# Running the delta rule's chunk scan between the levels of the block inverses, one chunk per level

## Chip, cores and metric

The kernel runs on one core of one Trainium2 chip, as one launch. The time is device microseconds (us) of the whole program, the median over several executions.

## What is computed

The program is one inference step of a hybrid encoder trunk with two layers, for 512 prompt frames and 64 sample frames at once (576 columns). Layer 0 is: SwiGLU feed-forward, then a mixer of 4 gated-delta heads and 4 latent-attention heads, then a second feed-forward. Layer 1 has a state-space mixer in place of the first. The change lies in the gated-delta part of the mixer. It works in chunks of 64 frames: 8 of the prompt, whose state starts at zero, and one of the sample, whose state is an input. The reference for one chunk, for all heads:

```python
def gdn_chunk_step(s0, inp):
    q, k, v, beta, g = inp
    ...
    sol = lax.linalg.triangular_solve(lower + jnp.eye(C, dtype=lower.dtype), rhs,
                                      left_side=True, lower=True, unit_diagonal=True)
    dv = v.shape[-1]
    u = sol[..., :dv] - jnp.einsum('bhtk,bhkv->bhtv', sol[..., dv:], s0)
    o = (gam[..., None] * jnp.einsum('bhtk,bhkv->bhtv', q, s0)
         + jnp.einsum('bhts,bhsv->bhtv', jnp.einsum('bhtd,bhsd->bhts', q, k) * decay, u))
    g_end = G[..., -1:]
    s_new = (jnp.exp(g_end)[..., None] * s0
             + jnp.einsum('bhsk,bhsv->bhkv', jnp.exp(g_end - G)[..., None] * k, u))
    return s_new, o
```

The triangular solve needs no state and can be done for all chunks alike. `u`, `o` and `s_new` need the state that the chunk before left.

## The kernel before

Every engine has one instruction stream, written out by hand, and waits on semaphores; each engine runs its stream strictly in the order written. Around the change TensorE (PE) runs `gdn_tensor`, then `scan_tensor`, then `onorm_tensor`; VectorE (DVE) and ScalarE (ACT) run the functions of the same stages.

**The block inverses** (`gdn_tensor`, `gdn_scalar`, `gdn_vector`). The 576 frames are five blocks: four of 128 frames (two chunks each) and block 4 of 64 frames (the sample). `PAIRS_OF_BLOCKS` takes them as pair one (blocks 0 and 1), pair two (blocks 2 and 3) and block 4 alone. For each block `gram` builds products and transposes, and the inverse of the block's triangular matrix is built in `LEVELS = 6` levels. In a level from 1 to 5, for each block of the pair, `first_product` (L1045) multiplies on PE, ACT copies the result to SBUF (`ys`, L1110), `updates` (L1054, L1058) multiplies again, and DVE subtracts from two running matrices and makes the mask product of the next level (`xi`, `zi`, `cm`: L1182, L1183, L1159). PE issues the first products of both blocks, then the updates of both. The last level leaves L1058 out. Then `solution` (L1073, L1075) makes what the scan needs, into PSUM banks 3 and 4, and ACT copies it out as `uv` and `wt` (L1115, L1116). The levels use banks 5 to 7 for one block of the pair and 0 to 2 for the other; `gram` uses banks 0 to 4.

**The scan** (`scan_tensor`, `scan_vector`, `scan_scalar`) starts when all blocks are done (`all_blocks_done`). For each of nine chunks, with four heads in each group of matmuls: L1214 multiplies `wt` with the state `st`; DVE makes `uu` from it (L1242); L1222 starts the chunk's output from the state; L1225 multiplies `kd` with `uu`; DVE makes the next state (L1247, four instructions); L1229 adds the rest of the output; ACT copies the output to `og` (L1265). Two sets of banks alternate from chunk to chunk (0 and 1, 2 and 3, 4 and 5). The trace counts each float32 matmul twice, so four heads stand as x8.

```python
            pe.wait_ge(s_st, c + 1)
...
            for h in range(HEADS):
                m = pe.matmul(ps[r0:r0 + CH, c % 2, h * P:h * P + P], wt[:, 4 * b + h, r0:r0 + CH], st[:, s, h, :],
                              start=True, stop=True)
```

`st` and `uu` lie over arrays of the first block set, which is why the scan waits for all blocks, and GpSimd (POOL) loads the sample's state into `st` after the blocks too (L827). After the scan, `onorm_*` normalises `og`, and latent attention, the output projection and the rest of the trunk follow.

Of the kernel before, what the change touches and what calls it, by code (L numbers as in the profile page):

```python
# [17 lines left out]
F32 = mybir.dt.float32  # L18
# [5 lines left out]
P = 128  # L24
# [15 lines left out]
NS = 3  # L40
# [70 lines left out]
def trunk(nc, i, o):  # L111
# [640 lines left out]
    assert RM0 + 2 * BYTES <= W0 and 2 * BYTES <= 2 * PADW * 4 and BYTES <= TOKENS * 4  # L752
    st = nc.alloc_sbuf_tensor_at("st", [P, 2, HEADS, P], F32, offset=KP0)
    uu = nc.alloc_sbuf_tensor_at("uu", [P, 2, HEADS, P], F32, offset=KP0 + 4096)
    rn = nc.alloc_sbuf_tensor_at("rn", [P, TOKENS], F32, offset=KP0 + 4096)
# [63 lines left out]
    def mix_gpsimd(pool):  # L819
        wait_u(pool, 1)  # L820
        pool.dma_start(xp[:, :, SEQ + 3:SEQ + 6], i["conv_state"]).then_inc(s_mc, 16)
        pool.dma_start(ckv[:, TOKENS:KEYS], i["cache_latent"]).then_inc(s_mk, 16)
        pool.wait_ge(s_evac, g_in + 6)
        pool.dma_start(o["conv_p"], xp[:, :, SEQ:SEQ + 3]).then_inc(s_out, 16)
        pool.dma_start(o["conv_s"], xp[:, :, PADW - 3:PADW]).then_inc(s_out, 16)
        all_blocks_done(pool)
        pool.dma_start(st[:, 1, :, :], i["gdn_state"]).then_inc(s_s0, 16)  # L827
        pool.wait_ge(s_st, 10)
        pool.dma_start(o["gdn_p"], st[:, 0, :, :]).then_inc(s_out, 16)
        pool.dma_start(o["gdn_s"], st[:, 1, :, :]).then_inc(s_out, 16)  # L830
        mla_gpsimd(pool)
# [175 lines left out]

    def all_blocks_done(eng):
        eng.wait_ge(s_bd[0], 3)
        eng.wait_ge(s_bd[1], 2)  # L1010

    def gdn_tensor(pe):
# [105 lines left out]
    def gdn_vector(dve):  # L1118
# [67 lines left out]

        for blocks in PAIRS_OF_BLOCKS:
# [12 lines left out]
    def chunk(c):  # L1200
        b = c // 2
        r0 = (c % 2) * CH
        return b, r0, 1 if c == 8 else 0

    def scan_tensor(pe):
        all_blocks_done(pe)
        for c in range(9):
            b, r0, s = chunk(c)
            tok = slice(c * CH, c * CH + CH)
            pe.wait_ge(s_st, c + 1)  # L1210
            if c == 8:
                pe.wait_ge(s_s0, 16)
            for h in range(HEADS):
                m = pe.matmul(ps[r0:r0 + CH, c % 2, h * P:h * P + P], wt[:, 4 * b + h, r0:r0 + CH], st[:, s, h, :],  # L1214
                              start=True, stop=True)
            m.then_inc(s_sw, 1)
            if c >= 2:
                pe.wait_ge(s_oc, c - 1)
            out = lambda h: ps[:, 2 + c % 2, h * CH:h * CH + CH]

            for h in range(HEADS):
                pe.matmul(out(h), st_old(c)[:, h, :], qg[:, h, tok], start=h == 0, stop=False)  # L1222
            pe.wait_ge(s_su, c + 1)
            for h in range(HEADS):
                m = pe.matmul(bank(4 + c % 2)[:, h, :], kd[r0:r0 + CH, 4 * b + h, :], uu[r0:r0 + CH, c % 2, h, :],  # L1225
                              start=True, stop=True)
            m.then_inc(s_ku, 1)
            for h in range(HEADS):
                m = pe.matmul(out(h), uu[r0:r0 + CH, c % 2, h, :], pt[r0:r0 + CH, 4 * b + h, r0:r0 + CH],  # L1229
                              start=False, stop=h == HEADS - 1)  # L1230
            m.then_inc(s_so, 1)

    def scan_vector(dve):
        all_blocks_done(dve)
        dve.memset(st[:, 0, :, :], 0.0).then_inc(s_st, 1)
        for c in range(9):
            b, r0, s = chunk(c)
            dve.wait_ge(s_sw, c + 1)
            if c >= 2:
                dve.wait_ge(s_so, c - 1)  # L1240
            rows_ = slice(r0, r0 + CH)
            dve.tensor_tensor(uu[rows_, c % 2, :, :], uv[rows_, 4 * b:4 * b + 4, :],  # L1242
                              ps[rows_, c % 2, :].rearrange("p (h c) -> p h c", h=HEADS),
                              ALU.subtract).then_inc(s_su, 1)
            dve.wait_ge(s_ku, c + 1)
            for h in range(HEADS):
                ins = dve.scalar_tensor_tensor(out=st[:, s, h, :], in0=st[:, s, h, :], scalar=ge[:, h, c:c + 1],  # L1247
                                               in1=bank(4 + c % 2)[:, h, :], op0=ALU.mult, op1=ALU.add)
            ins.then_inc(s_st, 1)
            if c == 7:  # L1250
                dve.wait_ge(s_s0, 16)
            if c < 8:
                dve.wait_ge(s_st, c + 2)
        dve.wait_ge(s_st, 10)
# [4 lines left out]
    def scan_scalar(act):  # L1259
        act.activation(zg[:, :, :], zg[:, :, :], ACT.Silu).then_inc(s_zs, 1)  # L1260
        for c in range(9):
            act.wait_ge(s_so, c + 1)
            if c == 0:
                all_blocks_done(act)
            act.activation(og[:, :, c * CH:c * CH + CH],  # L1265
                           ps[:, 2 + c % 2, 0:HEADS * CH].rearrange("p (h t) -> p h t", h=HEADS),
                           ACT.Copy).then_inc(s_oc, 1)

# [1100 lines left out]
```

## Time and profile before

| what | value |
|---|---|
| median of 3 runs | 2725.94 us (2725.25 to 2735.22) |
| the profiled execution's own time | 2718.02 us |
| its span, first to last instruction | 2716.4 us |
| PE busy | 2520.6 us, 93% of the span |
| DVE, ACT, POOL busy | 1467.3, 705.3, 134.0 us |
| mean granted clock of PE | 0.937 of full speed |
| block inverses, pair one / pair two / block 4 | about 688 to 748, 748 to 817, 817 to 855 us |
| chunk scan | 855 to 923 us |

The profile gives for each engine the time in which it ran instructions. In the page, a line of 40 digits cuts the span into 40 slices of 68 us; PEclk is the share of full clock that PE was granted in each. "PE 128*128 128x128" is a matmul whose weights are 128 rows by 128 columns and whose moving operand is 128 rows by 128 columns; PEld is the weight load that goes with it and overlaps it. A bracket such as [0.76 <-DVE cm L1159] says how long the engine had been idle before that row and which instruction released it.

### The profile page before, as it was taken

Reading aid. Unit: us, or ns where it says so; the run is one execution under the profiler, and the core shown is the slowest. Engines: PE = TensorE matmul, PEld = TensorE weight load, DVE = VectorE, ACT = ScalarE, POOL = GpSimd, SP = SyncE. Lnnn points to the kernel's source line nnn. Section 1 sums busy time; section 2 is a strip of 40 time slices with the busy share of each in tenths; the row PEclk is TensorE's granted clock in tenths of the full one; section 3 lists DMA queues with packets and bytes.
Section 4 is the critical chain, followed back from the end, with each engine's and each line's share of the span. In section 5 each row is a group of like instructions: output and inputs, shape, how many; then the busy total and the mean of one; then the engine's idle time right before and its main releaser. Section 6 shows DMA issues by size and latency. Waiting matters only on the chain.

```text
span 2716.4 us, 40923 instructions
## 1 busy us (share of the span) xinstructions
PE 2520.6 (93%) x18002; PEld 2407.2 (89%) x18002; DVE 1467.3 (54%) x2370; ACT 705.3 (26%) x940; POOL 134.0 (5%) x199
## 2 busy tenths in 40 slices
PE   6999999997777889999999999999977999999997
PEld 6999999995666656899999999999966889999996
DVE  4677664752552333586367487677765436333333
ACT  3121211533111132421121241222243315111112
POOL 2000000200000000100000020000000002000001
PEclk9999999997785568999999999999988999999998
DMA  6445442220000001244334234333324212222211
GB/s 266 167 152 194 176 154 74 80 75 16 1 1 4 23 18 62 70 172 168 111 140 153 91 131 177 107 139 137 126 76 124 65 63 78 93 70 86 93 59 55
DMA packets 55871, 275.07 MB, mean 101 GB/s; under 512 B 7216, under 2 KB 17008, under 8 KB 33040
## 3 DMA queue, kind: packets, MB, share of 16 engines
q1 hardware_dynamic: 40608, 186.35, 19.6%
q0 software_dynamic: 13648, 82.82, 8.6%
q8 instruction: 141, 2.31, 0.3%
q10 hardware_dynamic: 1440, 3.32, 0.3%
q14 instruction: 34, 0.28, 0.0%
HBM read 259.13 MB, written 13.32 MB: 100 GB/s over the span
## 4 chain that ended last, share of the span: by engine, by line
PE 60%; DVE 4%; ACT 1%; issue 1%; DMA 1%; SPq 1%; POOL 0%; ACTq 0%; DVEq 0%
PE ps L271 47%; PE ps L278 3%; PE ps L489 2%; PE ps L472 1%; DVE x L589 1%; PE ps L1395 1%; PE ps L1225 1%; PE ps L1214 1%; PE ps L1222 1%; PE ps L1394 1%; SPq L1687 1%; PE ps L1229 1%; DMA wm<-output_matrices 1%; DVE ln_rstd_tail L585 1%; PE ps L1416 0%
## 5 line engine op out<-in xcount | busy, mean ns | idle before, releaser
L271 PE MATMUL ps<-u_hi,w_hi 128*128 128x288 f32 x3040 | 648.5, 295 | 2.4 <-DVE w_lo L263 1.4
L271 PE MATMUL ps<-u_hi,w_lo 128*128 128x288 f32 x3040 | 647.2, 294 | 0.0
L271 PE MATMUL ps<-u_lo,w_hi 128*128 128x288 f32 x3040 | 647.0, 294 | 0.0
L263 DVE TENSOR_TENSOR w_lo<-w_raw,w_hi 128x2048 fp32r<-128x2048 f32 (+3 forms) x184 | 360.6, 1960 | 389.1 <-ACT w_hi L255 385.0
L255 ACT ACTIVATE w_hi<-w_raw 128x2048 fp32r<-128x2048 f32 (+3 forms) x184 | 303.4, 1649 | 897.2 <-DMA w_raw<-in_w_in 421.0
L271 PEld LDWEIGHTS ps<-u_hi,w_hi 128*128 128x128 f32 x3040 | 488.3, 188 | 3.2 <-DVE w_lo L263 1.6
L271 PEld LDWEIGHTS ps<-u_lo,w_hi 128*128 128x128 f32 x3040 | 488.0, 188 | 0.0
L271 PEld LDWEIGHTS ps<-u_hi,w_lo 128*128 128x128 f32 x3040 | 487.9, 188 | 0.0
L611 DVE SCALAR_TENSOR_TENSOR ada_out<-ada_w,c_act 128x1024 f32<-128x1024 f32 x272 | 317.0, 1221 | 28.9 <-DMA ada_w<-in_w_ada 26.9
L271 PE MATMUL ps<-h_lo,w_hi 128*128 128x288 f32 x1392 | 293.5, 295 | 0.0
L271 PE MATMUL ps<-h_hi,w_hi 128*128 128x288 f32 x1296 | 281.2, 298 | 4.8 <-DVE h_lo L1886 4.8
L271 PE MATMUL ps<-h_hi,w_lo 128*128 128x288 f32 x1296 | 276.7, 295 | 0.0
L415 DVE TENSOR_TENSOR hf<-ps,sg 128x576 f32<-128x576 f32 x88 | 66.6, 757 | 298.3 <-ACT sg L398 298.3
L271 PEld LDWEIGHTS ps<-h_lo,w_hi 128*128 128x128 f32 x1392 | 222.7, 189 | 0.0
L271 PEld LDWEIGHTS ps<-h_hi,w_hi 128*128 128x128 f32 x1296 | 210.0, 189 | 7.1 <-DVE h_lo L1886 5.0
L271 PEld LDWEIGHTS ps<-h_hi,w_lo 128*128 128x128 f32 x1296 | 208.6, 189 | 0.0
L398 ACT ACTIVATE sg<-ps 128x576 f32<-128x576 f32 x88 | 57.2, 650 | 488.1 <-PE ps L271 479.2
L441 DVE SCALAR_TENSOR_TENSOR x<-ps,res_gate,x 128x224 f32<-128x224 f32 (+2 forms) x240 | 85.9, 412 | 118.5 <-PE ps L271 95.2
L278 PE MATMUL ps<-u_hi,w_hi 128*128 128x288 f32 x352 | 109.4, 311 | 8.2 <-POOL u_lo L553 8.2
L278 PE MATMUL ps<-u_lo,w_hi 128*128 128x288 f32 x352 | 104.7, 297 | 0.0
L278 PE MATMUL ps<-u_hi,w_lo 128*128 128x288 f32 x352 | 104.7, 297 | 0.0
L553 POOL TENSOR_TENSOR u_lo<-u_f,u_hi 128x288 fp32r<-128x288 f32 x80 | 70.8, 899 | 440.5 <-ACT u_hi L532 438.7
(376 smaller groups left out, 2707.4 us busy)
## 6 DMA issues: line engine op xcount, KB each, us to landing
w_raw<-in_w_in SPq DMA_DIRECT2D x88, 1024.0 KB, 4.8
ada_w<-in_w_ada POOLq DMA_DIRECT2D x64, 1024.0 KB, 4.9
w_raw<-in_w_out SPq DMA_DIRECT2D x32, 768.0 KB, 4.3
w_raw<-in_w_out SPq DMA_DIRECT2D x32, 640.0 KB, 3.8
w_raw<-in_w_mix_in SPq DMA_DIRECT2D x10, 1024.0 KB, 4.8
ada_w<-in_w_ada SPq DMA_DIRECT2D x8, 1024.0 KB, 26.2
output_matrices<-wm_new POOLq DMA_DIRECT2D x8, 576.0 KB, 3.2
wm<-output_matrices SPq DMA_DIRECT2D x8, 576.0 KB, 5.0
```

The costliest lines, as they stand in the source:

```text
L255: act.activation(w_hi[:, g % NS, 0:WIDTH[g]], w_raw[:, g % NS, 0:WIDTH[g]], ACT.Copy).then_inc(s_whi, 1)
L263: dve.tensor_tensor(w_lo[:, g % NS, 0:WIDTH[g]], w_raw[:, g % NS, 0:WIDTH[g]], w_hi[:, g % NS, 0:WIDTH[g]].bitcast(F32), ALU.subtract).the ...
L271: m = pe.matmul(out[:, a, :], w, mv[:, a, :], start=start and n_ == 0, stop=stop and n_ == 2)
L278: m = pe.matmul(out, w, mv, start=start and n_ == 0, stop=stop and n_ == 2)
L398: act.activation(halves(sg[:, b % 2, :]), pair(2 * (b % 2)), ACT.Silu).then_inc(s_sg, 1)
L415: dve.tensor_tensor(halves(hf[:, b % 2, :]), pair(2 * (b % 2) + 1), halves(sg[:, b % 2, :]), ALU.mult).then_inc(s_evac, 1)
L441: return dve.scalar_tensor_tensor(out=x[:, b, lo:hi], in0=pair(2 * (b % 2))[:, a, lo - a * HALF:hi - a * HALF], scalar=res_gate[:, site, b ...
L472: return pe.matmul(pair(1)[:, a, :], mean_w[:, :], half(x, k, a), start=k == 0, stop=k == KD - 1)
L489: pe.matmul(pair(3)[:, a, :], mean_w[:, :], sq[:, k % SQ, :], start=k == 0, stop=k == KD - 1).then_inc(s_var, 1)
L553: pool.tensor_tensor(half(u_lo, k, a), half(u_f32, k, a), half(u_hi, k, a).bitcast(F32), ALU.subtract).then_inc(s_up, 1)
L585: chains["dve"].step(dve.reciprocal(ln_rstd[:, a, :], ln_std[:, a, :]))
L611: return dve.scalar_tensor_tensor(out=ada_out[:, n % 2, :], in0=w, scalar=1.0, in1=c_act[:, st, :], op0=ALU.mult, op1=ALU.mult, accum_out= ...
```

## The change

The scan is cut into `chunk_state` (L1214 and L1222 of before), `chunk_update`, `chunk_output` (L1225 and L1229 of before), `chunk_next_state` and `chunk_copy`. Chunks 0 to 3 run in levels 1 to 4 of pair two, chunks 4 to 7 in levels 1 to 4 of block 4: on PE the chunk's first half stands between the first products and the updates, its second half after the updates. On DVE `uu` stands before the level's subtractions and the new state after them; on ACT the copy stands after the level's copies. Chunk 8 (the sample) stays behind the last solution. All chunks use bank 3 (state product, then outer product) and bank 4 (output), which the levels leave alone; `solution` waits for the chunks before it writes there. `st` and `uu` move to the upper halves of a weight slot that holds a narrow block at that time, so the state is cleared and the sample's state loaded before the blocks instead of after them.

```diff
-    st = nc.alloc_sbuf_tensor_at("st", [P, 2, HEADS, P], F32, offset=KP0)
-    uu = nc.alloc_sbuf_tensor_at("uu", [P, 2, HEADS, P], F32, offset=KP0 + 4096)
+    M_SLOT = (first["mla"] + 1) % NS
...
+    st = nc.alloc_sbuf_tensor_at("st", [P, 2, HEADS, P], F32, offset=W0 + (M_SLOT + 1) * BLOCK * 4 - 2 * BYTES)
+    uu = nc.alloc_sbuf_tensor_at("uu", [P, 2, HEADS, P], F32, offset=W0 + (NS + M_SLOT + 1) * BLOCK * 4 - 2 * BYTES)
...
-        all_blocks_done(pool)
+        pool.wait_ge(s_blk, g_mla)
         pool.dma_start(st[:, 1, :, :], i["gdn_state"]).then_inc(s_s0, 16)
...
+    def scan_beside(j, lv):
+
+        return 4 * (j - 1) + lv - 1 if j and lv <= 4 else None
+
+    def block_of_chunk_done(eng, c):
+        b = c // 2
+        eng.wait_ge(s_bd[b % 2], b // 2 + 1)
...
         def solution(b, n_, paired):
...
+            if j:
+                pe.wait_ge(s_st, 4 * j + 1)
+                pe.wait_ge(s_oc, 4 * j)
...
             for lv in range(1, LEVELS):
+                c = scan_beside(j, lv)
                 for b, t0, n_ in blocks:
                     first_product(b, n_, lv)
+                if c is not None:
+                    if lv == 1:
+                        pe.wait_ge(s_kv[blocks[-1][0] % 2], j + 1)
+                    chunk_state(pe, c)
                 for b, t0, n_ in blocks:
                     updates(b, n_, lv)
+                if c is not None:
+                    chunk_output(pe, c)
...
+                if scan_beside(j_, lv) is not None:
+                    chunk_copy(act, scan_beside(j_, lv))
...
+        dve.wait_ge(s_blk, g_mla)
+        dve.memset(st[:, 0, :, :], 0.0).then_inc(s_st, 1)
...
             for lv in range(1, LEVELS):
+                c = scan_beside(j, lv)
+                if c is not None:
+                    chunk_update(dve, c)
                 for b, t0, n_ in blocks:
                     update(b, n_, lv)
                     if lv + 1 < LEVELS:
                         part(b, n_, lv + 1)
+                if c is not None:
+                    chunk_next_state(dve, c)
...
+    def chunk_state(pe, c):
+        b, r0, s = chunk(c)
+        tok = slice(c * CH, c * CH + CH)
+        block_of_chunk_done(pe, c)
+        pe.wait_ge(s_st, c + 1)
+        if c == 8:
+            pe.wait_ge(s_s0, 16)
+        for h in range(HEADS):
+            m = pe.matmul(ps[r0:r0 + CH, 3, h * P:h * P + P], wt[:, 4 * b + h, r0:r0 + CH], st[:, s, h, :],
+                          start=True, stop=True)
+        m.then_inc(s_sw, 1)
+        if c >= 1:
+            pe.wait_ge(s_oc, c)
+        for h in range(HEADS):
+            pe.matmul(chunk_out(h), st_old(c)[:, h, :], qg[:, h, tok], start=h == 0, stop=False)
...
     def scan_tensor(pe):
-        all_blocks_done(pe)
-        for c in range(9):
...
+        chunk_state(pe, 8)
+        chunk_output(pe, 8)
```

What this does to the order, at three places. In the rows, names with a number such as `zi_120` belong to the second block of the pair.

PE, one level of pair two, before (first products, updates):

```order
L1045 MATMUL ps<-zi,cm 128x128 x4
L1045 MATMUL ps<-zi_120,cm_122 128x128 x4
L1054 MATMUL ps<-ys,xi 128x128 x4
L1058 MATMUL ps<-xi,ys 128x128 x4
L1054 MATMUL ps<-ys_121,xi_119 128x128 x4
L1058 MATMUL ps<-xi_119,ys_121 128x128 x4
```

and now, with the line numbers of the changed kernel:

```order
L1052 MATMUL ps<-zi,cm 128x128 x4
L1052 MATMUL ps<-zi_120,cm_122 128x128 x4
L1239 MATMUL ps<-st,wt 64x128 x4
L1245 MATMUL ps<-qg,st 128x64 x4
L1061 MATMUL ps<-ys,xi 128x128 x4
L1065 MATMUL ps<-xi,ys 128x128 x4
L1061 MATMUL ps<-ys_121,xi_119 128x128 x4
L1065 MATMUL ps<-xi_119,ys_121 128x128 x4
L1254 MATMUL ps<-uu,kd 128x128 x4
L1258 MATMUL ps<-pt,uu 128x64 x4
```

Sixteen matmuls of a chunk stand inside the level, eight ahead of the updates and eight behind them.

DVE, the same level of pair two, now:

```order
L1269 TENSOR_TENSOR uu<-uv,ps 64x512
L1201 TENSOR_TENSOR xi<-xi,ps 128x512
L1202 TENSOR_TENSOR zi<-zi,ps 128x512
L1178 TENSOR_TENSOR cm<-dl,masks 128x512
L1201 TENSOR_TENSOR xi_119<-xi_119,ps 128x512
L1202 TENSOR_TENSOR zi_120<-zi_120,ps 128x512
L1178 TENSOR_TENSOR cm_122<-dl_118,masks 128x512
L1278 SCALAR_TENSOR_TENSOR st<-st,ge,ps 128x128 x4
```

The six rows in the middle are the level as it was; the first row and the last (four instructions) are the chunk's.

PE, one level of block 4, the last solution and the end of the scan, now:

```order
L1052 MATMUL ps<-zi,cm 64x64 x4
L1239 MATMUL ps<-st,wt 64x128 x4
L1245 MATMUL ps<-qg,st 128x64 x4
L1061 MATMUL ps<-ys,xi 64x64 x4
L1065 MATMUL ps<-xi,ys 64x64 x4
L1254 MATMUL ps<-uu,kd 128x128 x4
L1258 MATMUL ps<-pt,uu 128x64 x4
...
L1083 MATMUL ps<-vp,zi 64x128 x4
L1085 MATMUL ps<-zi,kp 128x64 x4
L1239 MATMUL ps<-st,wt 64x128 x4
L1245 MATMUL ps<-qg,st 128x64 x4
L1254 MATMUL ps<-uu,kd 128x128 x4
L1258 MATMUL ps<-pt,uu 128x64 x4
```

Before, a level of block 4 had its three groups alone, and nine chunks followed the last solution instead of one.

## Rows read from the trace of the kernel before

**Rows 1.** The page: granted clock by slice, and the chain that ended last.

```profile
PEclk9999999997785568999999999999988999999998
...
PE ps L271 47%; PE ps L278 3%; PE ps L489 2%; PE ps L472 1%; DVE x L589 1%; PE ps L1395 1%; PE ps L1225 1%; PE ps L1214 1%; PE ps L1222 1%; PE ps L1394 1%; SPq L1687 1%; PE ps L1229 1%; DMA wm<-output_matrices 1%; DVE ln_rstd_tail L585 1%; PE ps L1416 0%
```

**Rows 2.** Busy time by stretch: us, PE, PEld, DVE, ACT, POOL, PEclk, DMA share, GB/s.

```profile
771.70:782.00 10.30, 7.67 (x34) 7.38 (x35) 5.31 (x12) 1.19 (x2) 0.00 (x0) 0.50 0.00 0
782.00:817.20 35.20, 28.39 (x232) 26.50 (x231) 16.83 (x26) 6.95 (x12) 0.00 (x0) 1.00 0.00 1
819.50:855.40 35.90, 21.11 (x144) 17.90 (x142) 12.74 (x43) 3.42 (x9) 0.00 (x0) 0.50 0.00 0
855.40:923.40 68.00, 66.64 (x288) 61.51 (x288) 16.76 (x46) 6.90 (x13) 1.16 (x3) 0.50 0.01 4
```

**Rows 3.** The chain in order of time, one chunk of the scan: start us, us, what.

```profile
863.74 1.90 PE ps L1214 x8
865.64 1.90 PE ps L1222 x8
867.54 2.00 PE ps L1225 x8
869.54 1.60 PE ps L1229 x8
871.14 1.90 PE ps L1214 x8
```

**Rows 4.** Timeline of the same chunk, DVE and ACT: start us, us, what, idle before.

```profile
865.75 0.69 DVE L1242 TENSOR_TENSOR uu<-uv,ps 64x512 f32<-64x512 f32 x1 [2.44 <-PE ps L1214]
...
869.58 1.12 DVE L1247 SCALAR_TENSOR_TENSOR st<-st,ge,ps 128x128 f32<-128x128 f32 x4 [3.14 <-PE ps L1225]
...
871.18 0.38 ACT L1265 ACTIVATE og<-ps 128x256 f32<-128x256 f32 x1 [7.02 <-PE ps L1229]
```

**Rows 5.** Timeline, from the last block to the scan.

```profile
855.08 0.36 ACT L1116 ACTIVATE wt<-ps 128x256 f32<-128x256 f32 x1
...
856.30 1.94 PE L1214 MATMUL ps<-st,wt 128*64 128x128 f32 x8 [1.75 <-DVE st L1235]
```

**Rows 6.** Timeline, level 2 of pair two and the start of level 3.

```profile
786.90 1.16 PE L1045 MATMUL ps<-zi,cm 128*128 128x128 f32 x8 [0.76 <-DVE cm L1159]
787.89 1.06 PE L1054 MATMUL ps<-ys,xi 128*128 128x128 f32 x8
...
788.79 1.06 PE L1058 MATMUL ps<-xi,ys 128*128 128x128 f32 x8
...
789.88 0.69 DVE L1182 TENSOR_TENSOR xi<-xi,ps 128x512 f32<-128x512 f32 x1 [3.04 <-PE ps L1058]
...
793.87 1.16 PE L1045 MATMUL ps<-zi,cm 128*128 128x128 f32 x8 [0.76 <-DVE cm L1159]
```

**Rows 7.** Timeline, level 1 of pair two.

```profile
778.11 2.07 PE L1045 MATMUL ps<-zi,cm 128*128 128x128 f32 x8 [0.50 <-DVE cm L1159]
...
779.97 1.92 PE L1054 MATMUL ps<-ys,xi 128*128 128x128 f32 x8
...
781.68 1.19 PE L1058 MATMUL ps<-xi,ys 128*128 128x128 f32 x8
```

**Rows 8.** Timeline, a level of block 4 and the start of the next.

```profile
833.00 1.11 PE L1045 MATMUL ps<-zi,cm 64*64 64x64 f32 x8 [1.29 <-DVE cm L1159]
...
834.58 1.11 PE L1054 MATMUL ps<-ys,xi 64*64 64x64 f32 x8 [0.47 <-ACT ys L1110]
...
835.49 1.06 PE L1058 MATMUL ps<-xi,ys 64*64 64x64 f32 x8
...
837.83 1.11 PE L1045 MATMUL ps<-zi,cm 64*64 64x64 f32 x8 [1.29 <-DVE cm L1159]
```

**Rows 9.** Timeline, weight loads of one line in the two blocks of pair two.

```profile
748.33 0.96 PEld L1024 LDWEIGHTS ps<-gcum,ident 4*128 4x128 f32 x8 [1.43 <-issue]
...
761.62 1.78 PEld L1024 LDWEIGHTS ps<-gcum,ident 4*128 4x128 f32 x8 [1.84 <-issue]
```

More of the change, by code:

```diff
@@ L752, in trunk @@
     assert RM0 + 2 * BYTES <= W0 and 2 * BYTES <= 2 * PADW * 4 and BYTES <= TOKENS * 4
-    st = nc.alloc_sbuf_tensor_at("st", [P, 2, HEADS, P], F32, offset=KP0)
-    uu = nc.alloc_sbuf_tensor_at("uu", [P, 2, HEADS, P], F32, offset=KP0 + 4096)
+    M_SLOT = (first["mla"] + 1) % NS
+    assert WIDTH[first["mla"] + 1] * 4 + 2 * BYTES <= BLOCK * 4
+    st = nc.alloc_sbuf_tensor_at("st", [P, 2, HEADS, P], F32, offset=W0 + (M_SLOT + 1) * BLOCK * 4 - 2 * BYTES)
+    uu = nc.alloc_sbuf_tensor_at("uu", [P, 2, HEADS, P], F32, offset=W0 + (NS + M_SLOT + 1) * BLOCK * 4 - 2 * BYTES)
     rn = nc.alloc_sbuf_tensor_at("rn", [P, TOKENS], F32, offset=KP0 + 4096)
@@ L812, in trunk @@
     g_in = first["mix_in"]
+    g_mla = first["mla"]
     def mix_sync(sp):
@@ L1006, in level_banks @@
         return (5, 6, 7) if w == 0 else (0, 1, 2)
-    def all_blocks_done(eng):
-        eng.wait_ge(s_bd[0], 3)
-        eng.wait_ge(s_bd[1], 2)
+    def scan_beside(j, lv):
[3 more added lines that the diff above has]
+        eng.wait_ge(s_bd[b % 2], b // 2 + 1)
     def gdn_tensor(pe):
@@ L1078, in gdn_tensor @@
         pe.wait_ge(s_col, 1)
-        for blocks in PAIRS_OF_BLOCKS:
+        for j, blocks in enumerate(PAIRS_OF_BLOCKS):
             for b, t0, n_ in blocks:
@@ L1091, in gdn_scalar @@
     def gdn_scalar(act):
-        for blocks in PAIRS_OF_BLOCKS:
+        for j_, blocks in enumerate(PAIRS_OF_BLOCKS):
             for b, t0, n_ in blocks:
@@ L1185, in update @@
             dve.wait_ge(s_xz[w], LEVELS * j + lv + 1)
-        for blocks in PAIRS_OF_BLOCKS:
+        dve.wait_ge(s_blk, g_mla)
+        dve.memset(st[:, 0, :, :], 0.0).then_inc(s_st, 1)
+        for j, blocks in enumerate(PAIRS_OF_BLOCKS):
             for b, t0, n_ in blocks:
@@ L1203, in chunk @@
         return b, r0, 1 if c == 8 else 0
-    def scan_tensor(pe):
-        all_blocks_done(pe)
-        for c in range(9):
[L1208 to L1231, printed above, removed]
@@ L1233, in scan_vector @@
-    def scan_vector(dve):
[L1234 to L1253, printed above, removed]
+    def chunk_state(pe, c):
[13 more added lines that the diff above has]
+            pe.matmul(chunk_out(h), st_old(c)[:, h, :], qg[:, h, tok], start=h == 0, stop=False)
@@ new lines, in chunk_out, with chunk_output @@
+    def chunk_out(h):
+        return ps[:, 4, h * CH:h * CH + CH]
+    def chunk_output(pe, c):
+        b, r0, s = chunk(c)
+        pe.wait_ge(s_su, c + 1)
+        for h in range(HEADS):
+            m = pe.matmul(bank(3)[:, h, :], kd[r0:r0 + CH, 4 * b + h, :], uu[r0:r0 + CH, c % 2, h, :],
+                          start=True, stop=True)
+        m.then_inc(s_ku, 1)
+        for h in range(HEADS):
+            m = pe.matmul(chunk_out(h), uu[r0:r0 + CH, c % 2, h, :], pt[r0:r0 + CH, 4 * b + h, r0:r0 + CH],
+                          start=False, stop=h == HEADS - 1)
+        m.then_inc(s_so, 1)
@@ new lines, in chunk_update, with chunk_next_state @@
+    def chunk_update(dve, c):
+        b, r0, s = chunk(c)
+        block_of_chunk_done(dve, c)
+        dve.wait_ge(s_sw, c + 1)
+        if c >= 2:
+            dve.wait_ge(s_so, c - 1)
+        rows_ = slice(r0, r0 + CH)
+        dve.tensor_tensor(uu[rows_, c % 2, :, :], uv[rows_, 4 * b:4 * b + 4, :],
+                          ps[rows_, 3, :].rearrange("p (h c) -> p h c", h=HEADS), ALU.subtract).then_inc(s_su, 1)
+    def chunk_next_state(dve, c):
+        s = chunk(c)[2]
+        dve.wait_ge(s_ku, c + 1)
+        if c:
+            dve.wait_ge(s_st, c + 1)
+        for h in range(HEADS):
+            ins = dve.scalar_tensor_tensor(out=st[:, s, h, :], in0=st[:, s, h, :], scalar=ge[:, h, c:c + 1],
+                                           in1=bank(3)[:, h, :], op0=ALU.mult, op1=ALU.add)
+        ins.then_inc(s_st, 1)
@@ L1254, in scan_vector, with chunk_copy @@
+    def chunk_copy(act, c):
+        act.wait_ge(s_so, c + 1)
+        act.activation(og[:, :, c * CH:c * CH + CH],
+                       ps[:, 4, 0:HEADS * CH].rearrange("p (h t) -> p h t", h=HEADS), ACT.Copy).then_inc(s_oc, 1)
+    def scan_tensor(pe):
+        chunk_state(pe, 8)
+        chunk_output(pe, 8)
+    def scan_vector(dve):
+        chunk_update(dve, 8)
+        dve.wait_ge(s_s0, 16)
+        chunk_next_state(dve, 8)
         dve.wait_ge(s_st, 10)
@@ L1260, in scan_scalar @@
         act.activation(zg[:, :, :], zg[:, :, :], ACT.Silu).then_inc(s_zs, 1)
[L1261 to L1267, printed above, removed]
+        chunk_copy(act, 8)
     def onorm_scalar(act):
@@ L1338, in trunk @@
     s_pv = sem("values_weighted")
-    g_mla = first["mla"]
     UNITS = [(h, qb * P, P, 0, (qb + 1) * P) for qb in range(4) for h in range(HEADS)]
```

## The prediction, made before the run

> **What bounds the kernel now.** I read the page first. The chain that ended last lies mostly on PE, and the four lines of the scan (L1214, L1222, L1225, L1229) are each 1% of it [rows 1]. The digits of PEclk below 9 mark the mixer as the place where PE runs at a lower clock [rows 1]. Next I cut the mixer into stretches [rows 2]. In the scan PE is busy 66.64 of 68.00 us at a granted clock of 0.50, which is 1.2 GHz, from start to end. Pair two of the block inverses has two parts: until 782 us it runs at 0.50, and from there to 817 us at 1.00 (2.4 GHz) with PE busy 28.39 of 35.20 us. Block 4 runs at 0.50 with PE busy 21.11 of 35.90 us. So the scan is bound by PE at its lower clock, and the two stages into which the chunks move leave PE idle for a fifth and for two fifths of their time. What a chunk costs there depends on how much of that idle time it finds and on the clock it is granted.
>
> **What is taken away.** In the scan a chunk repeats every 871.14 - 863.74 = 7.40 us, and the chain stays on PE through all four lines [rows 3]. DVE's `uu` (0.69), its new state (1.12) and ACT's copy (0.38) lie beside it [rows 4]. Eight of the nine chunks leave: 8 x 7.40 = 59.2. Chunk 8 stays and I leave its 7.40 as it is, at the clock of the scan. In front of the scan `wt` is copied by 855.44 and the first matmul starts at 856.30 because DVE still has to clear `st` [rows 5]; the clearing now lies before the blocks, where DVE waits for the first gram, and I leave 0.1 for the handoff: 0.8 saved. Together **-60.0 us**.
>
> **What is added to pair two.** A level now takes 793.87 - 786.90 = 6.97 us, and groups of eight matmuls follow each other at 788.79 - 787.89 = 0.90 us [rows 6]. There are six such groups in it (two first products, four updates), 5.4 us. DVE makes the other half of the loop: it waits 3.04 us for the updates, and PE 0.76 us for `cm` [rows 6]. No row shows a chunk's matmuls at 2.4 GHz. At the least they halve, 3.70. The nearest row is a line with a narrow operand at both clocks, the weight loads of L1024: 0.96 us for eight at the higher and 1.78 at the lower [rows 9], a factor of 0.54, which gives 7.40 x 0.54 = 4.0. I take 3.9, nearer to the measured pair. PE then has 5.4 + 3.9 = 9.3 us to issue in a level, more than the old loop, so PE sets the pace: +2.3 a level, 7.0 for three levels.
>
> The first of the four levels starts at 1.2 GHz [rows 2]. There a group of eight takes 781.68 - 779.97 = 1.71 us [rows 7]. From the second first product at 778.11 [rows 7] PE would reach the chunk at 779.82. If the clock rises at 782 as before, L1214 ends at 781.72, L1222 at about 782.85, the four updates take 3.6, the chunk's second half 1.9 and the next first product 0.9: the next level begins at 789.25 instead of 786.90, +2.4. If the whole of the chunk's first half and the updates runs at 1.2 GHz, 779.82 + 3.80 + 4 x 1.71 + 2.8 gives 793.3, +6.4. I take 3.5, since the updates are the same 128 x 128 matmuls after which the clock rose before, and only the 3.8 us of the chunk stand ahead of them. Pair two: 7.0 + 3.5 = **+10.5** (8.7 to 13.6).
>
> **What is added to block 4.** A level takes 837.83 - 833.00 = 4.83 us and has three groups at 835.49 - 834.58 = 0.91 each [rows 8], 2.7 us of PE. The chunk adds its 7.40 at the clock that this stretch has: 10.1 us on PE. What DVE and ACT do in a level, 4.83 - 2.7 = 2.1, now lies beside the chunk's matmuls, so PE alone sets the pace: +5.3 for each of four levels, **+21.2**. A change of shape between groups could add up to 0.2 at three places a level, which nothing in the rows excludes, +2.4 at most.
>
> **What I cost at nothing.** DVE's `uu` and new state are 1.81 us in 3.04 us of idle time of a pair-two level [rows 4, 6]; in block 4 DVE is busy 12.74 of 35.90 us [rows 2]. Uncovered they would cost those 1.81 us a level. A new wait stands on PE before L1214: the chunk's state comes from DVE after `cm`, and behind the wait are queued the updates, for which ACT and DVE wait in turn. The second first product (0.90) and PE's backlog cover the 1.12 us of the state, at most 0.3 a level is bare. One output bank instead of two makes L1222 wait for ACT's 0.38 us copy of the chunk before; a first product stands between. The waits in `solution` come a whole level after their chunks. The load of the sample's state moves from after the blocks to before them on POOL's queue, where the next instruction waits for the end of the scan anyway; SP's queue is not touched.
>
> **The sum.** -60.0 + 10.5 + 21.2 = -28.3 us. Against the profiled execution's own 2718.02 that is 2689.7. That execution lies 7.9 below the median of the runs, so I apply the difference to the median: 2725.94 - 28.3 = **2697.6 us**. The bounds above give -30 to -23; the later stages, where the clock also changes level [rows 1], are shifted in time and may gain or lose some us, and the three runs before lie 10 us apart. So the forecast's own range is 2689 to 2708.
>
> **The clock, and a rule about it.** The scan shows PE busy 98% of 68 us and still at 0.50, in every stretch I looked at [rows 2]. The Trainium skill (TensorE: Matmul & The Clock Gate, section "What's actually happening") says that the throttled state is the default and that sustained activity of the engine releases it. By that rule the scan would have run at 2.4 GHz, which the trace contradicts; by it block 4, once filled with chunks, would too.
>
> **Rivals.**
> Block 4 gains the higher clock. For it: PE's idle time there goes, and chunk groups of 128 rows stand next to the level's own. Against it: the scan, the same chunk work without any pause, stayed at 0.50 [rows 2], and block 4's own matmuls are 64 x 64 [rows 8]. A level would be 3.9 + 1.4 = 5.3 us instead of 10.1, 19 less for four, and chunk 8 about 3 less: 2676. This is the rule of the page just named. Chance 0.12.
>
> The chunk's matmuls do not speed up with the clock, being held by weight loads or the change of shape. Then a pair-two level is 5.4 + 7.4 = 12.8, +5.8 each, 23 in place of 10.5: -16, 2710. The row of L1024, which nearly halves [rows 9], speaks against it. Chance 0.08.
>
> Pair two loses the higher clock: chunk work, which ran at 0.50 in the scan, sits in every level, and the clock does not rise during the first. It decides if the updates of the first two levels do not bring it back. A level is then 6 x 1.71 + 7.40 = 17.7, +10.7 for three of them and 17.7 - 8.79 = +8.9 for the first (8.79 from 778.11 to 786.90 [rows 6, 7]); level 5 and the two solutions, eight groups, lose 0.8 each, 6.4. So -60.0 + 41.0 + 6.4 + 21.2 = +8.6, **slower**: 2734.5. Against it: in the old level 1 the clock rose right after groups of just these updates, at 1.2 GHz, and held through gaps of 0.76 us [rows 6, 7]; the new levels have fewer gaps. Chance 0.06.
>
> That the chunks do not move at all is excluded by the written order; PE runs it as it stands.
>
> **How the numbers follow.** The forecast has 0.70, the rivals 0.12, 0.08 and 0.06, and 0.04 is for later stages moving by over 10 us. From the bottom, 2676 takes in half of the first rival, and 2712 the second; left out are the slower rival, the rest of the first and the tails. About 0.5% (13.6 us) is what a measurement can tell from no change. Faster by more than that are the forecast but for its tail (0.68), the first rival (0.12) and most of the second (0.06): 0.86. Same: the rest of the second, most of the slower rival and the tails, 0.11. Slower by more: 0.03.
>
> **What would show it.** Behind the last solution one chunk of 7.4 us instead of nine, and the first matmul of it 0.1 us after the copy of `wt`. Levels 2 to 4 of pair two repeat every 9.3 us at clock 1.00, with PE hardly idle; levels 1 to 4 of block 4 every 10.1 us at 0.50. DVE's new state should start while PE is still in the chunk's last group. The forecast is wrong if the granted clock in pair two is 0.50 beyond its second level, if it is 1.00 in block 4, or if the two paces differ from these by over 1 us with PE waiting for `st` in between.

## The result, and the profile after

The changed kernel takes **2691.31 us** (median of four runs, 2680.72 to 2704.04), the kernel before, beside it, 2728.13 (four runs, 2725.25 to 2735.22). The ratio is 0.9863, 95% interval 0.9815 to 0.9911: faster by 0.9 to 1.9%, or 24 to 50 us. The forecast was 2697.6 us, and "faster by over 0.5%" with a chance of 0.86.

The profiled execution took 2689.28 us (span 2687.5), 28.7 less than the profiled execution before. The page after, PE's clock by slice and the chain that ended last, which answer to [rows 1]:

```profile
PEclk9999999997886769999999999999988999999998
...
PE ps L271 48%; PE ps L278 5%; PE ps L489 2%; PE ps L472 1%; PE ps L1052 1%; PE ps L1061 1%; PE ps L1429 1%; DVE x L589 1%; PE ps L1428 1%; DMA wm<-output_matrices 1%; PE ps L1065 1%; PE ps L1239 1%; PE ps L1254 1%; PE ps L1245 1%; SPq L1721 0%
```

The dip in the clock is shorter by a digit. The chunk's lines (L1239, L1245, L1254) are still in the chain, and the levels' lines (L1052, L1061, L1065) have joined them: in a level PE now goes from one to the other without a pause.

To see where the time went I cut the delta rule's stage at four instructions of PE: the first gram of pair one (L1024 before, L1031 after), the first gram of pair two, the first gram of block 4, and the first matmul of the output norm (L1290, L1325). Pair one starts here at its gram, at 675.8 us before, and not at its first product at 688. Busy time in these three pieces, before (us, PE, PEld, DVE, ACT, POOL, PEclk, DMA share, GB/s):

```profile
675.80:748.40 72.60, 53.59 (x337) 50.00 (x337) 38.88 (x90) 11.64 (x20) 0.00 (x0) 0.79 0.00 1
748.40:817.30 68.90, 49.27 (x337) 46.03 (x337) 38.80 (x90) 11.64 (x20) 0.00 (x0) 0.83 0.00 1
817.30:924.20 106.90, 89.95 (x456) 81.48 (x457) 30.13 (x91) 11.51 (x23) 1.63 (x3) 0.51 0.01 4
```

The same pieces after:

```profile
667.60:740.00 72.40, 53.41 (x336) 49.88 (x337) 39.35 (x91) 11.64 (x20) 0.00 (x0) 0.79 0.00 1
740.00:819.50 79.50, 64.13 (x465) 60.11 (x465) 45.65 (x110) 13.18 (x24) 0.00 (x0) 0.85 0.00 1
819.50:888.90 69.40, 60.10 (x328) 54.36 (x329) 22.40 (x70) 9.99 (x19) 1.07 (x2) 0.51 0.01 2
```

Pair one stays (-0.2), pair two grows by 10.6, block 4 with the scan shrinks by 37.5: together -27.1 us. PE's busy time, the number behind the length of the stretch, splits that. In the stage it falls from 192.8 to 177.6, by 15.2: the last piece loses 29.85 us of it (89.95 - 60.10), four chunks, and pair two gains 14.86 (64.13 - 49.27), because nearly all of their work runs at twice the clock there. The rest, 11.9 us, is idle time of PE that is gone: 4.3 in pair two (19.6 to 15.4) and 7.65 in block 4 with the scan (16.95 to 9.30). The four chunks in block 4 run at 0.50 as they did in the scan, so they gain idle time only.

Of the -28.7 us of the profiled pair 27.1 are thus in this stage, and 1.6 are a sum of larger differences elsewhere, which the last section comes back to.

### The profile page after: what moved, and what is told of

Its sections match the earlier page's. It is cut to its first block, busy times and chain, and to the rows that moved or that the text cites. A ratio compares the mean times of both kernels' runs of the same rounds, so it can differ in the third digit from the quotient of the medians.

```text
span 2687.5 us, 40939 instructions
## 1 busy us (share of the span) xinstructions
PE 2503.3 (93%) x18002; PEld 2392.2 (89%) x18002; DVE 1466.7 (55%) x2370; ACT 705.2 (26%) x940; POOL 133.5 (5%) x199
## 4 chain that ended last, share of the span: by engine, by line
PE 66%; DVE 5%; issue 1%; ACT 1%; DMA 1%; SPq 0%; POOL 0%; DVEq 0%; ACTq 0%
PE ps L271 48%; PE ps L278 5%; PE ps L489 2%; PE ps L472 1%; PE ps L1052 1%; PE ps L1061 1%; PE ps L1429 1%; DVE x L589 1%; PE ps L1428 1%; DMA wm<-output_matrices 1%; PE ps L1065 1%; PE ps L1239 1%; PE ps L1254 1%; PE ps L1245 1%; SPq L1721 0%
## 5 line engine op out<-in xcount | busy, mean ns | idle before, releaser
L611 DVE SCALAR_TENSOR_TENSOR ada_out<-ada_w,c_act 128x1024 f32<-128x1024 f32 x272 | 317.0, 1220 | 28.7 <-DMA ada_w<-in_w_ada 26.8
```

Of the source, the lines that this page charges most:

```text
L611: return dve.scalar_tensor_tensor(out=ada_out[:, n % 2, :], in0=w, scalar=1.0, in1=c_act[:, st, :], op0=ALU.mult, op1=ALU.mult, accum_out= ...
```

## The experiments

The theory: the chunks cost what PE's clock makes of them where they land, PE sets the pace of every level that holds one, and DVE and ACT are covered. Rivals: DVE's additions set the pace; the gain is the early state or the handoff, not the levels; and, behind these, the scan's slow clock is no property of the chunks but of how PE enters them, so that the same gain was to be had without moving anything. A kernel that was executed once or twice is compared by the stage and its three pieces, since whole times of one kernel lie up to 23 us apart. The last four columns of the table are the distances between the cuts named above, in one profiled execution each.

| kernel | whole time, us | stage | pair one | pair two | block 4 + scan |
|---|---|---|---|---|---|
| before | 2718.02 | 248.4 | 72.6 | 68.9 | 107.0 |
| after | 2689.28 | 221.4 | 72.5 | 79.5 | 69.4 |
| changed_again | 2686.77 | 217.7 | 71.0 | 77.9 | 68.8 |
| state_early | 2716.37 | 244.6 | 69.3 | 69.3 | 106.1 |
| pair_only | 2713.26 | 226.3 | 69.4 | 80.0 | 76.9 |
| double_uu | 2697.39 | 221.3 | 72.4 | 79.5 | 69.4 |
| warm_scan | 2713.59 | 242.9 | 71.1 | 67.2 | 104.6 |
| warm_block4 | 2694.48 | 212.8 | 69.3 | 79.8 | 63.7 |
| rows_only | 2702.71 | 217.2 | 70.8 | 76.5 | 69.9 |
| warm_scan_rows | 2687.93 | 220.2 | 70.7 | 67.2 | 82.3 |
| warm_block4_rows | 2651.20 | 194.8 | 69.3 | 78.5 | 47.0 |
| warm_all_rows | 2650.68 | 184.8 | 64.4 | 72.1 | 48.3 |

The kernel before took 2737.41 us beside pair_only, double_uu, warm_scan and warm_block4, 2738.33 beside state_early and rows_only, and 2716.66 (median of seven, 2711.95 to 2734.52) beside the other four. On PE pair one is the same program in all but the last row and still varies by 3.3 us, with the moment at which the clock rises in it; a difference of that size in one execution says nothing.

### pair_only: chunks 0 to 3 in pair two, the rest behind the blocks

```diff
-        return 4 * (j - 1) + lv - 1 if j and lv <= 4 else None
+        return 4 * (j - 1) + lv - 1 if j == 1 and lv <= 4 else None
...
-        chunk_state(pe, 8)
-        chunk_output(pe, 8)
+        pe.wait_ge(s_bd[0], 3)
+        for c in range(4, 9):
+            chunk_state(pe, c)
+            chunk_output(pe, c)
```

> Chunks 0 to 3 stay beside pair two, chunks 4 to 8 run behind block 4. Measured from the first gram matmul to the first matmul of the output norm the delta stage took 248.4 us before and 221.4 with the change. Theory (PE's time sets every pace; in pair two a chunk costs little because PE has 2.4 GHz there): pair two as in the changed kernel, 9.6 us a level; block 4 back at 4.83 a level; five chunks of 7.40 behind it; stage 228 to 230, so pair two alone brings about 19 of the 27 us. Rival (the gain is PE's idle time, filled): pair two has 1.6 us idle a level and block 4 has 2.1, so pair two alone brings about 12, stage about 237.

Measured: a stage of 226.3 us, 22.1 less than before and 4.9 more than after; 3 us of it are pair one. The pieces that the edit touches say it without that: pair two is 11.1 longer, block 4 with the scan 30.1 shorter, together -19.0, where the theory gave 19 and its rival 12. Chunks 4 to 7 in block 4 are worth the difference between 76.9 and 69.4, 7.5 us, which is the idle time of PE counted above (7.65). Pair two brings most of the gain, as argued.

### double_uu: DVE's subtraction done twice

```diff
+        chains["dve"].step(dve.tensor_tensor(
+            uu[rows_, c % 2, :, :], uv[rows_, 4 * b:4 * b + 4, :],
+            ps[rows_, 3, :].rearrange("p (h c) -> p h c", h=HEADS), ALU.subtract))
```

> The changed kernel, with DVE's subtraction for uu done twice in every chunk, 0.7 us more on DVE for each. Theory (PE sets the pace in both stages and DVE's part of a chunk is hidden): 9.6 and 10.3 us a level as before, stage 221 to 222. Rival (the chunk's chain through DVE sets the pace): 0.7 us more in each of eight levels and in chunk 8, stage about 227.

Measured: the stage is 221.3 us against 221.4. The timeline of DVE in a level of pair two of this kernel (start us, us, what, idle before):

```profile
791.50 0.69 DVE L1269 TENSOR_TENSOR uu<-uv,ps 64x512 f32<-64x512 f32 x1 [1.82 <-PE ps L1239]
792.22 0.69 DVE L1272 TENSOR_TENSOR uu<-uv,ps 64x512 f32<-64x512 f32 x1
794.30 0.69 DVE L1201 TENSOR_TENSOR xi<-xi,ps 128x512 f32<-128x512 f32 x1 [1.39 <-PE ps L1065]
```

The second subtraction takes 0.7 us of DVE's wait and leaves 1.39. On PE that level goes from 788.39 to 797.98, 9.59 us, exactly as without it. DVE's `uu` is covered; its new state and ACT's copy were not lengthened in any kernel.

### state_early: the kernel before with only the new places and the early state

The edit is the part of the diff on `st` and `uu`, the early `memset` and POOL's earlier wait; the scan stays behind the blocks.

> The kernel before with only the new places of st and uu, the state cleared and the sample's state loaded before the blocks; the nine chunks stay in a row behind the blocks. Theory: the first chunk starts right after the last copy, 0.7 us less, and nothing else: stage 247 to 248 against 248.4.

Measured: block 4 with the scan is 0.9 us shorter; the first chunk starts at 853.51, 0.04 behind the end of the `wt` copy, where it was 0.86 [rows 5]:

```profile
853.51 1.97 PE L1218 MATMUL ps<-st,wt 128*64 128x128 f32 x8 [0.95 <-ACT wt L1118]
```

The other 3 us by which the stage is shorter are pair one, where the clock happened to rise 6 us earlier. The change's gain is not here.

### changed_again: the changed kernel, measured again beside others

> The changed kernel as it is, on the same chip and in the same rounds as warm_all_rows. Its stage is 221 to 222 us in every execution; its whole time against the kernel before is 24 to 40 us less, and what moves between executions lies outside this stage.

Measured: 2684.28 us (2681.14 to 2703.75, four runs), 0.9875 of before, interval 0.9812 to 0.9939: the result repeats. The stage is 217.7 in the execution that was profiled, below the 221 to 222 that was expected of every one; pair one (71.0) and pair two (77.9) make up most of the difference, with the moments at which the clock rises in them. So the stage itself moves by some 4 us from execution to execution.

### warm_scan: sixteen unread matmuls ahead of the old scan

```diff
     def scan_tensor(pe):
+        for _ in range(16):
+            pe.matmul(ps[:, 7, 0:P], ident[:, :], ident[:, :], start=True, stop=True)
         all_blocks_done(pe)
```

> The kernel before, with 16 matmuls of 128 x 128 by 128 that nobody reads put on PE between the last solution and the scan; the scan itself stays as it was, nine chunks in a row. Theory A (the chunk work can run at 2.4 GHz, and the old scan ran at 1.2 GHz because PE entered it there): granted clock 1.00 in the scan, a chunk about 4 us instead of 7.40, nine of them 31 us less, the added matmuls cost about 5; stage about 222 instead of 248.4. Theory B (chunk work in a row is always granted 1.2 GHz): the clock is back at 0.50 within the first two chunks, a chunk 7.40, stage 249 to 254.

Measured: a stage of 242.9 us, between the two theories. The clock rises while the sixteen matmuls run (841.7 to 847.4), and falls again after two chunks. By stretch:

```profile
841.70:847.40 5.70, 5.70 (x33) 5.58 (x32) 0.48 (x1) 4.26 (x4) 0.56 (x1) 0.64 0.17 46
847.40:856.20 8.80, 8.11 (x65) 7.35 (x64) 3.61 (x10) 0.67 (x2) 0.00 (x0) 0.99 0.01 2
856.20:908.10 51.90, 51.84 (x224) 47.86 (x224) 12.64 (x36) 2.40 (x7) 0.12 (x1) 0.50 0.00 1
```

Two chunks take 4.42 us each, then the rest 7.4 as before, with PE busy in practically every microsecond. So the slow scan was not slow because chunks cannot run at 2.4 GHz: it was entered at 1.2 and stayed there. But chunks in a row did not keep the higher clock here either. Block 4 with the scan is only 2.4 us shorter than before; the other 3 us of the stage are the two pairs, which the edit does not touch.

### warm_block4: unread matmuls around block 4's gram

```diff
+                if b == 4:
+                    fill(5)
                 gram(b, t0, n_)
+                if b == 4:
+                    fill(20)
                 first_product(b, n_, 0)
+                if b == 4:
+                    fill(5)
```

Here and below `fill(n)` is n times the matmul of warm_scan.

> The changed kernel, with matmuls of 128 x 128 by 128 that nobody reads put on PE where it idles around block 4's gram: 5 before it, 20 after it, 5 before the first product of level 1. Theory A (block 4 with its chunks can hold 2.4 GHz if PE comes into it at 2.4 GHz): granted clock 1.00 through block 4, a level about 5.3 us instead of 10.33, the last solution and chunk 8 faster too; stage about 196 instead of 221.4. Theory B (this mixture of work is granted 1.2 GHz whatever came before): 0.50 from the first level on, 10.3 us a level, stage 221 to 225.

Measured: a stage of 212.8 us, again between the theories. Here the unread matmuls did not raise the clock: it was 1.00 since the first level of pair two, and with them it did not fall in block 4's first part. That part, block 4's level 1 and what follows, by stretch:

```profile
824.40:835.90 11.50, 10.88 (x102) 10.13 (x100) 8.22 (x32) 2.19 (x5) 0.00 (x0) 1.00 0.00 0
835.90:841.50 5.60, 5.58 (x56) 5.21 (x56) 2.39 (x7) 0.38 (x1) 0.00 (x0) 1.00 0.02 4
841.50:872.60 31.10, 31.10 (x171) 28.62 (x170) 9.38 (x26) 2.29 (x6) 0.00 (x0) 0.50 0.00 1
```

Level 1 with its chunk takes 5.7 us at clock 1.00, then the clock falls although PE has no idle time at all. Without the unread matmuls, in the change, all four of block 4's levels with chunks ran at 0.50 (the row 830.60 to 872.00 further below).

### rows_only, warm_scan_rows, warm_block4_rows: the chunk's second half on all 128 rows

A chunk uses 64 of the 128 rows of `kd`, `pt` and `uu`. These kernels let the last two groups of chunks 0 to 7 take all 128, with the other half of `uu` set to zero once; the number of matmuls and the size of their outputs stay.

```diff
+        dve.memset(uu[0:CH, 1, :, :], 0.0)
+        dve.memset(uu[CH:P, 0, :, :], 0.0)
...
+        rows_ = slice(0, P) if c < 8 else slice(0, CH)
...
-            m = pe.matmul(bank(3)[:, h, :], kd[r0:r0 + CH, 4 * b + h, :], uu[r0:r0 + CH, c % 2, h, :],
+            m = pe.matmul(bank(3)[:, h, :], kd[rows_, 4 * b + h, :], uu[rows_, c % 2, h, :],
...
```

rows_only has this alone, in the changed kernel:

> The changed kernel with the second half of chunks 0 to 7 on all 128 rows and no added matmuls: the control for warm_block4_rows (stage 194.8 us) and warm_block4 (212.8). Theory (the clock that block 4 is entered with decides, the rows only help to hold it): granted clock 0.50 in block 4's levels, 10.3 us each, pair two 9.3 a level; stage 217 to 221. Rival (the rows alone bring the higher clock): about 5.7 us a level in block 4, stage 197 to 202.

warm_scan_rows has it in the old scan, with the sixteen unread matmuls:

> As warm_scan, where the scan's first two chunks ran at 1.00 and took 4.4 us each and the others 7.40 at 0.50; in addition the second half of a chunk takes all 128 rows for chunks 0 to 7. Theory A: 1.00 through the eight chunks, 4.4 us each; against warm_scan six chunks save 3.0 each, stage 242.9 - 18 = 225, close to the 221 of the changed kernel although every chunk still stands behind the blocks. Theory B: the clock falls after two chunks as before, stage 242 to 244.

warm_block4_rows has it in the changed kernel, with the unread matmuls of warm_block4:

> As warm_block4, in which the granted clock held 1.00 through level 1 of block 4 and fell in level 2; in addition the two matmul groups of a chunk's second half take all 128 rows (the other half of uu is cleared once and stays zero) for chunks 0 to 7. Theory A (the level fell short of 1.00 because of its 64-row groups): 1.00 through the four levels, 5.7 us a level as in level 1 of warm_block4 instead of 10.3, the last solution also faster; stage 192 to 198 instead of 212.8. Theory B (rows make no difference): the clock falls in level 2 again, stage 212 to 214.

Measured. In rows_only block 4 stays at the lower clock, all 41 us of the levels that hold chunks; the rows alone do nothing there:

```profile
836.00:877.00 41.00, 41.00 (x224) 37.79 (x223) 11.87 (x32) 2.94 (x8) 0.00 (x0) 0.50 0.00 1
```

In warm_scan_rows the clock rises at 859.2, while the unread matmuls run (855.1 to 860.8), and it holds for all nine chunks of the old, serial scan, of which the first eight have 128 rows:

```profile
847.00:859.20 12.20, 10.13 (x51) 9.31 (x52) 2.87 (x7) 4.36 (x5) 0.56 (x1) 0.50 0.08 21
859.20:892.00 32.80, 30.16 (x248) 27.72 (x248) 12.65 (x35) 2.97 (x8) 0.00 (x0) 1.00 0.01 1
892.00:900.00 8.00, 6.84 (x56) 6.33 (x56) 3.62 (x10) 1.10 (x3) 0.17 (x1) 1.00 0.01 2
```

The stage is 220.2 us, as short as the change makes it (221.4, 217.7), **without moving one chunk**; 24.7 us of the difference to before lie in block 4 with the scan, the rest in the two pairs, which the edit does not touch. A chunk takes 4.3 us here, of which PE waits 0.38 for the state from DVE, a wait that the interleaved levels don't have (timeline, the last unread matmuls and the first matmuls of two chunks):

```profile
858.66 2.20 PE L1207 MATMUL ps<-ident 128*128 128x128 f32 x16
860.78 1.09 PE L1216 MATMUL ps<-st,wt 128*64 128x128 f32 x8
...
865.07 1.09 PE L1216 MATMUL ps<-st,wt 128*64 128x128 f32 x8 [0.38 <-DVE st L1252]
```

In warm_block4_rows the levels of block 4 hold 1.00 too:

```profile
835.00:858.00 23.00, 22.53 (x228) 20.70 (x227) 11.52 (x32) 3.07 (x9) 0.00 (x0) 1.00 0.00 1
```

A level of block 4 takes 5.66 us there instead of 10.33, and the stage falls to 194.8. With both the higher clock and the interleaving the stage is 25 us shorter than the serial one at the higher clock (194.8 against 220.2). How much of that is interleaving stays open: warm_block4_rows also runs block 4's own matmuls at 1.00, and warm_scan_rows runs them at 0.50. The old scan with 128 rows and no unread matmuls was not run.

### warm_all_rows: the same, with unread matmuls at every gram

```diff
                 gram(b, t0, n_)
+                fill(20 if b == 4 else 18)
```

Beside this, `fill(5)` stands ahead of the grams of blocks 2 and 4 and behind the first products of blocks 0, 2 and 4.

> As warm_block4_rows, with the unread matmuls also in the idle time of PE around the gram of the other four blocks (18 after each gram, 5 more where PE waits before the next). Theory: the clock stays at 1.00 from the gram of block 0 to the last chunk; the gram, first products and first level of pair one and pair two run at 2.4 GHz, some 2 to 3 us less for each block; stage 180 to 190. Rival: the added matmuls run at 0.50 at their first places and push the first products back, 2 to 4 us each; stage 195 to 205. Whole time: 30 to 40 us below the changed kernel by the theory.

Measured: 2647.91 us (2643.78 to 2651.92, four runs), **0.9721 of before**, interval 0.9672 to 0.977, where the changed kernel beside it stood at 0.9875. Pair one and pair two in this kernel:

```profile
681.00:740.60 59.60, 49.51 (x409) 46.76 (x408) 36.84 (x83) 11.05 (x19) 0.00 (x0) 1.00 0.00 1
740.60:812.70 72.10, 65.50 (x556) 62.89 (x557) 45.59 (x110) 13.18 (x24) 0.00 (x0) 1.00 0.00 1
```

The clock stays at 1.00 from 681 to 848 us, so the last chunk, the sample's, still runs at 0.50. The stage is 184.8 us, within the 180 to 190 of the theory, and the median is 36 us below the changed kernel's, with no overlap of the runs (2651.92 at most against 2681.14 at least).

## Why the prediction was right

**The chunks removed** (-60.0): from the end of the `wt` copy to the end of the last copy of `og` 67.9 us became 7.9, -60.0. The handoff is part of it; timeline of its two rows, to be read beside [rows 5]:

```profile
879.75 0.36 ACT L1135 ACTIVATE wt<-ps 128x256 f32<-128x256 f32 x1
...
880.16 1.97 PE L1239 MATMUL ps<-st,wt 128*64 128x128 f32 x8 [0.95 <-ACT wt L1135]
```

PE starts 0.05 us behind the copy.

**Pair two** (+10.5): measured +10.6, partly by luck, since two errors cancel: levels 2 to 4 cost 7.9 (3 x 2.62) where 7.0 was forecast, and the first level 2.7 where 3.5 was taken. One level of it in the chain in order of time (start us, us, what):

```profile
780.28 1.98 PE ps L1052 x16
782.27 1.02 PE ps L1239 x8
783.28 1.04 PE ps L1245 x8
784.32 0.95 PE ps L1061 x8
785.26 0.89 PE ps L1065 x8
786.16 0.89 PE ps L1061 x8
787.05 0.89 PE ps L1065 x8
787.95 1.09 PE ps L1254 x8
789.03 0.84 PE ps L1258 x8
789.87 1.98 PE ps L1052 x16
```

PE goes through the level without a wait, in 9.59 us where 9.3 was predicted. A chunk costs 1.02 + 1.04 + 1.09 + 0.84 = 3.99 (predicted 3.9); the other 0.2 are the two first products, 1.98 instead of 1.80. The narrow weight loads of [rows 9] were the right row to scale by: 3.99 to 7.40 is the factor 0.54 that they gave, and 4.0 would have been nearer than the 3.9 that was taken. The first level:

```profile
769.73 2.07 PE ps L1052 x8
771.80 1.89 PE ps L1239 x8
773.70 1.03 PE ps L1245 x8
```

Here the clock rose during the chunk's first half, before any update of the level had run: L1239 takes 1.89, L1245 1.03. So the reason that the forecast gave for its 3.5, that the updates bring the clock up, is not what happened. The level, from the second first product at 769.73 to that of the next level at 781.2, takes 11.5 us against 8.79: +2.7, at the lower end of the 2.4 to 6.4 given. The rival in which pair two loses the higher clock fell with this row; in the rest of pair two the granted clock is 1.00 throughout, and in block 4 it is 0.50 with PE busy in practically every microsecond. Both by stretch:

```profile
780.30:818.20 37.90, 36.59 (x304) 34.66 (x304) 19.40 (x40) 7.40 (x14) 0.00 (x0) 1.00 0.00 1
830.60:872.00 41.40, 41.38 (x225) 38.17 (x225) 11.88 (x32) 2.66 (x7) 0.00 (x0) 0.50 0.00 1
```

One reading of the forecast was too broad: pair two before did not run at 0.50 all the way to 782 us. From 748.3 to 771.7 its mean clock was 0.71, and the row of L1024 at 748.33 in [rows 9], at the higher clock, lies in that part. The sum used only the level from 778.11, where 0.50 is right.

**Block 4** (+21.2): measured +22.2 from the first product of level 1 to the solution (22.58 became 44.76). One level:

```profile
841.03 1.04 PE ps L1052 x8
842.07 1.90 PE ps L1239 x8
843.97 1.90 PE ps L1245 x8
845.87 1.04 PE ps L1061 x8
846.91 0.85 PE ps L1065 x8
847.76 2.00 PE ps L1254 x8
849.76 1.60 PE ps L1258 x8
851.36 1.04 PE ps L1052 x8
```

10.33 us against 10.1: the chunk is 7.40 as in [rows 3], and the level's own groups take 2.93 where [rows 8] gave 2.7. The "change of shape" that was bounded with 2.4 us for all levels is this 0.2 a level, at the most.

**What was costed at nothing** stayed at nothing: in the two stretches just shown PE waits once each, 1.3 us for `wt` between the two solutions and 1.4 us for `cm` ahead of the first level, as before the change (1.26 and 1.39). double_uu shows it for `uu` by an experiment. One sign was wrong in a detail: DVE's new state was to start while PE is in the chunk's last group. In block 4 it does; in pair two it does not. The new state in a level of each (timeline):

```profile
780.46 1.11 DVE L1278 SCALAR_TENSOR_TENSOR st<-st,ge,ps 128x128 f32<-128x128 f32 x4
...
849.80 1.12 DVE L1278 SCALAR_TENSOR_TENSOR st<-st,ge,ps 128x128 f32<-128x128 f32 x4 [0.81 <-PE ps L1254]
```

In pair two it starts 0.2 us behind the chunk's last group (PE is at the next level from 780.28), since DVE works off the level's subtractions first. It is done at 781.57, and PE needs it at 782.27: the 1.98 us of the two first products cover it, with 0.7 to spare, as the text said of the backlog.

**Size.** Terms of -60.0, +10.5 and +21.2 became -60.0, +10.6 and +22.2, a sum of -27.2 against -28.3; the stage as a whole says -27.1. The medians differ by 36.8. The profiled execution before lies 10.1 below the median of the four runs beside the change, the one after only 2.0 below its own. So the other ten are, as far as the profiles show, spread from execution to execution, of which the last section describes a part; the runs that were not profiled can't be split into stages. On the size of the step the prediction is right by the profiles and short by the medians; 2691.31 lies within its range, and -28 within the interval of 24 to 50 us.

**The clock.** The likeliest rival was that block 4, once filled, gains 2.4 GHz. It did not: PE was busy 41.38 of 41.40 us there at a granted clock of 0.50. The Trainium skill (TensorE: Matmul & The Clock Gate, section "What's actually happening") has activity release the throttle. In warm_scan and warm_scan_rows it agrees: the clock rose while 16 plain 128 x 128 matmuls ran. In the change it does not: 41 us of chunk and level work left it at 0.50. In the kernels with unread matmuls around the grams these did not raise the clock but stood where it would have fallen; in warm_all_rows it rose at 681, within the first gram and before the first unread matmul (682.4).

Once at 1.00, the chunks kept the clock where their second half takes 128 rows (warm_scan_rows, warm_block4_rows, warm_all_rows) and lost it where it takes 64 (warm_scan, warm_block4), with PE busy 92% or more of the stretches shown in each, so busy time as the profile counts it does not tell these cases apart. In pair two, between the level's 128 x 128 matmuls, chunks with 64 rows kept it too. Each of the four kernels that are compared has one profile, and the two with 64 rows ran on another chip than the two with 128; that the rows decide rests on both pairs coming out the same way, and on warm_all_rows, whose mean granted clock is 0.963 to 0.965 in all four runs. What property of the rows the clock follows was not isolated: the first half, which has 128 rows in every kernel, was left as it is.

What I had not weighed is the alternative. The forecast took the scan's 0.50 as given and asked where to move the chunks; the runs show that the gain of moving, 27 us, was also to be had in the old scan by entering it at the higher clock with second halves of 128 rows (28 us, 24.7 of them in the piece that was edited; entering it so with 64 rows, in warm_scan, gave 5.5 and 2.4). Both together, with block 4's own levels at the higher clock, bring 54 (248.4 to 194.8), and with the earlier blocks 64 (to 184.8).

## What to carry to other kernels

Before moving work under another stage, ask at which clock PE enters it: the old scan showed PE busy 98% at 0.50, and its work was not all that bound it. Some unread matmuls in idle time just ahead of such a stretch are a cheap test. Price moved matmuls at the clock of the place where they land, split the gain into clock and idle time filled (here 15.2 and 11.9 us), and check both by PE's busy time per stage. Narrow operands padded with zeros to 128 rows cost nothing here: a level of pair two takes 9.26 us in warm_all_rows and 9.59 in the change, both at 1.00. Together with the unread matmuls they went with a clock that held; alone, in rows_only, they left it at 0.50.

## What was not expected of the hardware

Where the granted clock is 1.00 and PE is busy without a gap, the feed-forward stages run at one of two paces. Two stretches of 80 us, before:

```profile
200.00:280.00 80.00, 80.00 (x602) 80.00 (x602) 62.61 (x103) 13.01 (x9) 4.22 (x8) 1.00 0.53 189
1240.00:1320.00 80.00, 80.00 (x617) 80.00 (x617) 48.35 (x71) 13.90 (x11) 2.65 (x5) 1.00 0.42 149
```

and after:

```profile
200.00:280.00 80.00, 80.00 (x618) 80.00 (x617) 62.59 (x103) 13.43 (x9) 4.75 (x9) 1.00 0.54 192
1240.00:1320.00 80.00, 80.00 (x602) 80.00 (x601) 34.44 (x51) 13.59 (x10) 1.06 (x2) 1.00 0.32 109
```

The first stretch has 602 or 618 matmuls, the second 617 or 602: some 2.6% between them, in code that no kernel here touched. In the profiled pair the first brought 8 us and the second gave 8 back. Over all twelve profiles of this study three of the four combinations occur (602 and 602 in pair_only and warm_block4, 618 and 602 in changed_again and warm_scan, 602 and 617 in state_early and warm_all_rows), the last two of them in kernels with the scan interleaved and in kernels with it behind the blocks. The change is the only kernel with two profiles, and it took the same two paces in both, so a tie to the kernel is not excluded. In size this would do for much of the spread of runs, 8 to 23 us for one kernel, which no unprofiled run can confirm. What sets the pace stays open: the granted clock, PE's busy share and the DMA share beside it do not tell the two apart.
